# Moving loads, small steps and PSUM banks in a hand-ordered two-block transformer kernel

## The reference, cut to what matters

```python
def first_block(x, mem, ...):
    x = x + 0.5 * rmsnorm(swiglu(rmsnorm(x, g), ffn1), g_post)           # ffn1
    h = rmsnorm(x, mix_pre_g)
    proj = h @ w_in                     # q, k, v, z, xbc, dt, gates
    a = diff_attention(q, k, v) @ w_branch_attn
    s = (ssd(xbc, dt) gated by z, normed) @ w_branch_ssd
    x = x + rmsnorm((gates * (a, s)) @ w_mix_out, mix_post_g)            # mix
    x = x + rmsnorm(cross_attention(rmsnorm(x), mem) @ xa_w_o, xa_post_g) # xa
    return x + 0.5 * rmsnorm(swiglu(rmsnorm(x, g), ffn2), g_post)        # ffn2

def second_block(x, ...):
    proj = rmsnorm(x) @ w_in_2
    k_spec = rfft(filters made by a small sine network times a decay)    # from constants and weights
    u_hy = (hyena: gated long convolutions with k_spec, by FFT) @ w_hy_out
    u_attn = (attention with low-rank q and kv * silu(z)) @ w_attn_out
    merged = sigmoid(gate_hy) * u_hy + sigmoid(gate_attn) * u_attn
    return x + merged @ w_out
```

## Time and profile before

| | us |
|---|---|
| median of 3 runs | 1153.08 (1152.91 to 1153.16) |
| the profiled execution | 1152.91 |
| its span, first to last instruction | 1151.1 |
| TensorE busy in it | 1136.1 |
| VectorE busy | 774.7 |
| ScalarE busy | 589.3 |

### The profile page before, as it was taken

How to read it: one execution, slowest core, us unless ns; L and a number is a source line. 1 busy time by engine, 2 the same in 40 slices (tenths; PEclk the granted TensorE clock), 3 DMA queues, 4 the chain that set the end, 5 groups by cost and what they waited for, 6 DMA issues and landing times.

```text
span 1151.1 us, 21065 instructions
## 1 busy us (share of the span) xinstructions
PE 1136.1 (99%) x8564; PEld 1060.2 (92%) x8564; DVE 774.7 (67%) x1097; ACT 589.3 (51%) x846; POOL 0.2 (0%) x4
## 2 busy tenths in 40 slices
PE   7999999999999999999999999999999999999998
PEld 6999998999999999999999997999999699989898
DVE  5665555858898967786777746555555656984664
ACT  5544345557754335787445544444443466554361
POOL 0000000000000000000000000000000000000000
PEclk8999999999999999999999999999999999999999
DMA  7665555455443355444555333555555336443241
GB/s 284 239 217 183 182 182 182 167 200 184 153 177 110 111 170 179 147 142 157 182 199 203 106 134 128 188 199 177 190 193 182 105 132 241 147 146 110 73 147 38
DMA packets 29120, 189.62 MB, mean 165 GB/s; under 512 B 3480, under 2 KB 4793, under 8 KB 7226
## 3 DMA queue, kind: packets, MB, share of 16 engines
q1 hardware_dynamic: 26432, 180.89, 45.6%
q10 hardware_dynamic: 2618, 7.72, 2.0%
HBM read 187.55 MB, written 1.05 MB: 164 GB/s over the span
## 4 chain that ended last, share of the span: by engine, by line
PE 91%; DVE 5%; ACT 2%; issue 1%; DMA 1%; ACTq 0%; DVEq 0%
PE bank L457 26%; PE bank L459 26%; PE bank L458 26%; PE bank L535 3%; PE bank L912 2%; DVE sb_ssd_conv L2084 1%; PE bank L755 1%; PE bank L1093 1%; PE bank L1081 1%; DVE sb_w_lo L1874 1%; DMA sb_cols<-in_cols 1%; PE bank L899 1%; PE bank L1115 1%; PE bank L1138 1%; PE bank L975 0%
## 5 line engine op out<-in xcount | busy, mean ns | idle before, releaser
L1874 DVE TENSOR_TENSOR sb_w_lo<-sb_w_raw,sb_w_hi 128x2048 fp32r<-128x2048 f32 x169 | 386.5, 2290 | 179.5 <-ACT sb_w_hi L1224 179.4
L457 PE MATMUL bank<-sb_hT_hi,sb_w_hi 128*128 128x256 f32 x1576 | 447.5, 284 | 1.7 <-DVE sb_hT_lo L1957 1.7
L458 PE MATMUL bank<-sb_hT_lo,sb_w_hi 128*128 128x256 f32 x1576 | 440.3, 279 | 0.0
L459 PE MATMUL bank<-sb_hT_hi,sb_w_lo 128*128 128x256 f32 x1576 | 440.3, 279 | 0.0
L1224 ACT ACTIVATE sb_w_hi<-sb_w_raw 128x2048 fp32r<-128x2048 f32 x169 | 322.6, 1910 | 86.0 <-PE bank L459 84.5
L457 PEld LDWEIGHTS bank<-sb_hT_hi,sb_w_hi 128*128 128x128 f32 x1576 | 295.8, 188 | 6.4 <-issue 3.3
L458 PEld LDWEIGHTS bank<-sb_hT_lo,sb_w_hi 128*128 128x128 f32 x1576 | 295.5, 187 | 2.6 <-issue 1.4
L459 PEld LDWEIGHTS bank<-sb_hT_hi,sb_w_lo 128*128 128x128 f32 x1576 | 295.8, 188 | 0.0
L1281 ACT ACTIVATE sb_ffn_gate<-sb_ffn_gate 128x256 f32<-128x256 f32 x44 | 18.4, 418 | 149.0 <-DVE sb_ffn_gate L1972 149.0
L457 PE MATMUL bank<-sb_w_hi,sb_hT_hi 128*128 128x256 f32 x256 | 73.2, 286 | 0.7 <-DVE sb_hT_lo L2586 0.3
L458 PE MATMUL bank<-sb_w_lo,sb_hT_hi 128*128 128x256 f32 x256 | 71.1, 278 | 0.0
(11 more groups left out here) (406 smaller groups left out, 1748.4 us busy)
## 6 DMA issues: line engine op xcount, KB each, us to landing
sb_w_raw<-in_w SPq DMA_DIRECT2D x169, 1024.0 KB, 5.0
sb_w_raw<-in_w SPq DMA_DIRECT2D x4, 256.0 KB, 7.4
sb_w_raw<-in_w SPq DMA_DIRECT2D x2, 512.0 KB, 8.8
sb_mem_xn<-in_mem ACTq DMA_DIRECT2D x1, 1024.0 KB, 7.5
sb_post_g<-in_ffn_post_g ACTq DMA_DIRECT2D x2, 512.0 KB, 5.1
sb_dft_f<-in_c_dft ACTq DMA_DIRECT2D x1, 1024.0 KB, 6.7
out<-sb_x SPq DMA_DIRECT2D x4, 256.0 KB, 2.2
sb_x<-in_x SPq DMA_DIRECT2D x1, 512.0 KB, 3.9
```

The lines of the kernel that those rows point to most:

```text
L457: pe.matmul(o, a_hi, b_hi, start=first, stop=False)
L458: pe.matmul(o, a_hi, b_lo, start=False, stop=False)
L459: return pe.matmul(o, a_lo, b_hi, start=False, stop=last)
L1874: tt(w_lo[b % STAGES][:], w_raw[b % RING][:], f32(w_hi[b % STAGES][:]), ALU.subtract).then_inc(w_lo_in, 1)
```

## The change

Nothing is computed that was not computed before. Edits, by place:

- Start: the second half of `x` is loaded by SyncE right behind the first, ahead of the weights, and no longer by ScalarE ahead of `cols`; five warm-up matmuls in place of two.
- ffn1's end: two of the four banks of `norm_turn(1)` change places.
- mix: the first sine step moves behind the conversions of the mixed columns, on VectorE and ScalarE; the second moves into `out_part`, behind its second block, and its matmul behind `mix1`. The taps use banks 3, 4, 5, 6, 3, 4 in place of 3, 4, 5, 6, 2, 0, and `raw_turn(3)` claims 5, 6, 3, 4. On ScalarE the sum of squares for the next norm and the load of the post-norm gain move ahead of the sixth tap's copy.
- xa: `filter_decay` moves from ahead of the softmax into the `out_part` behind it, after its first and second block. On ScalarE the same two steps of the next norm move ahead of `spectrum(1)`.
- Last stage: `mla_turn(7)` moves from between the halves of `hyo0` to behind them; on ScalarE the first sigmoid moves ahead of the copy `mPT7`; on VectorE the block conversion moves ahead of `at_scale(3)` and the first `wide_gate`; on ScalarE the conversion of block `out1` moves behind the first of the four `fin` steps.

```diff
@@ tensor: start, ffn1's end
-                    norm_turn(1, mem_xn, 1, (7, 0, 2, 1))
+                    norm_turn(1, mem_xn, 1, (7, 0, 1, 2))
...
-            stay_warm(zeros[:, 0:P], zeros[:], 2)
+            stay_warm(zeros[:, 0:P], zeros[:], 5)
@@ tensor: mix
-                if i in (0, 2):
-                    filter_hidden(i // 2)
+                if i == 0:
+                    filter_hidden(0)
...
             token_pair(("mix0", "mix1"), FIRST["mix_out"], mixed_hi, mixed_lo, mixed_ready)
+            filter_hidden(1)
...
-            xq = FIRST["xa_q"]
             for i in range(6):
-                filter_taps(i, (3, 4, 5, 6, xq % 3, (xq + 1) % 3)[i])
-            raw_turn(3, x_added(1))
+                filter_taps(i, 3 + i % 4)
+            raw_turn(3, x_added(1), (5, 6, 3, 4))
             for i in (6, 7):
-                filter_taps(i, 7 if i == 6 else (xq + 2) % 3)
+                filter_taps(i, 7 if i == 6 else (FIRST["xa_q"] + 1) % 3)
@@ tensor: ffn2, last stage
-            filter_spectrum(2, (FIRST["ffn2"] + 2) % 3)
+            filter_spectrum(2, (FIRST["ffn2"] + 1) % 3)
...
-                             between=(lambda: at_turn(3, 7)) if i == 9 else lambda: mla_turn(7))
-                if 1 <= i < MLA_HEADS:
+                             between=(lambda: at_turn(3, 7)) if i == 9 else None)
+                if 1 <= i <= MLA_HEADS:
                     mla_turn(i - 1)
@@ scalar: start, mix, xa
-            act.dma_start(x[:, 1, :], a["x"][P:SEQ, :]).then_inc(S("x_in1"), 16)
...
-                if i == 0:
-                    hidden_sin(0)
             after(FIRST["attn_out"] + 3)
-            hidden_sin(1)
+            hidden_sin(0)
...
-            out_part("mix_out", "mix", 1)
+            def mix_between(i):
+                if i == 1:
+                    hidden_sin(1)
+
+            out_part("mix_out", "mix", 1, mix_between)
...
-            for i in range(6):
+            for i in range(5):
                 taps(i)
+            post_gain(2, POST[2])
+
+            norm_squares(x, xa_xn)
+            taps(5)
             norm_high(3, "xa_pre_g", hT_hi)
             for i in range(6, 8):
                 taps(i)
-            post_gain(2, POST[2])
-
-            norm_squares(x, xa_xn)
...
             spectrum(0)
+            post_gain(3, POST[3])
+
+            norm_squares(x, ffn[2]["xn"])
             spectrum(1)
             norm_high(4, "ffn2_pre_g", hT_hi)
-            post_gain(3, POST[3])
-
-            norm_squares(x, ffn[2]["xn"])
@@ scalar: last stage (the sigmoid's five lines, moved up, and this)
-            after(FIRST["at_out"])
             for i in range(4):
...
                 act.activation(hT_hi[:, 2 * i:2 * i + 2, :], mg2[:, 2 * i:2 * i + 2, :], ACT.Copy).then_inc(S("fin_hi"), 1)
+                if i == 0:
+                    after(FIRST["at_out"])
@@ vector: mix, xa (out_part calls between(i) behind low_after(FIRST[stage] + i))
-                if i == 0:
-                    hidden_arg(0)
             low_after(FIRST["attn_out"] + 3)
-            hidden_arg(1)
-            out_part("mix_out", "mix", 1)
+            hidden_arg(0)
+
+            def mix_between(i):
+                if i == 1:
+                    hidden_arg(1)
...
-            for t in range(TOK):
-                filter_decay(t)
...
-            out_part("xa_o", "xo", 2)
+            def xo_between(i):
+                if i < 2:
+                    filter_decay(i)
@@ vector: last stage
+                low_after(FIRST["gate2"] + i)
                 if i == 8:
                     at_scale(3)
 
                     dve.wait_ge(S("gate2"), 1)
-                    wide_gate(0, True)
-                low_after(FIRST["gate2"] + i)
-                if i == 9:
-                    wide_gate(1, True)
+                if i >= 8:
+                    wide_gate(i - 8, True)
@@ sync
-            sp.dma_start(x[:, 0, :], a["x"][0:P, :]).then_inc(S("x_in0"), 16)
+            for t in range(TOK):
+                sp.dma_start(x[:, t, :], a["x"][t * P:(t + 1) * P, :]).then_inc(S(f"x_in{t}"), 16)
```

More of the change, by code:

```diff
@@ L1340, in ffn_part, with out_part @@
                 after(down_at(n, PAIRS - 1))
-            def out_part(stage, key, i_post):
+            def out_part(stage, key, i_post, between=None):
                 for i in range(3):
@@ L1352, in out_part @@
                     after(FIRST[stage] + i)
+                    if between:
+                        between(i)
                 for t in range(TOK):
@@ L1817, in _ @@
                     read(ins, f"gg{i}")
+                if i >= 8:
+                    for j in range(8):
+                        wait_read(act, f"gg{j}")
+                    c = slice(8 * (i - 8), 8 * (i - 7))
+                    act.activation(gate2[:, c, :], gate2[:, c, :], ACT.Sigmoid).then_inc(S("gate2"), 1)
                 if i == 0:
@@ L1822, in _ @@
                     copy(f"mPT{i - 1}", m_PT[:], two(o))
-                if i >= 8:
-                    for j in range(8):
-                        wait_read(act, f"gg{j}")
-                    c = slice(8 * (i - 8), 8 * (i - 7))
-                    act.activation(gate2[:, c, :], gate2[:, c, :], ACT.Sigmoid).then_inc(S("gate2"), 1)
                 if i < MLA_HEADS:
@@ L2408, in _ @@
             xa_low(3)
-            out_part("xa_o", "xo", 2)
+            def xo_between(i):
+                if i < 2:
+                    filter_decay(i)
+            out_part("xa_o", "xo", 2, xo_between)
             norm_low(4, "ffn2_pre_g", hT_hi, hT_lo)
```

## The result

The changed kernel takes 1164.55 us (median of 4 executions, 1163.23 to 1166.01), the kernel before in the same comparison 1153.12 (1152.91 to 1153.86): ratio 1.0098, 95% interval 1.0081 to 1.0115. The prediction was 1164.4, range 1158.5 to 1168.0. The executions of the changed kernel spread over 2.8 us and the profiled one, at 1168.75, is slower than all four; those of before lie within 1 us. That spread is part of the result, and the profile shown is one from its upper end.

What follows compares the result with a forecast made beforehand. TensorE, busy 1136.1 of 1151.1 us, was taken as the bound, its idle time mostly at the start. -1.2 + 0 + 5.1 + 2.0 + 2.7 = +8.6, with clock +2.9 +11.5, on 1152.91: 1164.4, range 1158.5 to 1168.0.

Steps and rivals of the forecast that it cites:

- The mechanism: Start: with `cols` and x's second half loaded sooner, the first norm columns come at 8.6 in place of 9.82.
- 7.1 to 7.6: Start, a sign to look for: ScalarE's first rounding at these times in place of 9.29.
- The zeros' end at 7.25: Start: ten warm-up records end then if the granted clock rises at about 4.5 us; at 10 us if late.
- The term -1.2: Start: gain in us from earlier loads, less three more warm-ups; bounds -2.1 to +0.2.
- the predicted +5.1: mix: us from turnings of `raw_turn(3)` held by the sixth tap's late copy; range +1.6 to +5.6.
- the releaser named: mix, a sign: TensorE's turnings released by ScalarE's `sb_kfil`; release by VectorE's `sb_x` would favour the third rival.
- The third rival: mix and xa: sixth and second copies don't hold the turnings, no clock fall; +3.7 us, 1156.6; chance 0.10.
- 1.7 taken: mix: us for a fallen clock behind the wait ahead of `raw_turn(3)`, half of 3 us and a bit.
- the upper bound of 3.4: mix and xa: most that a fallen clock would cost behind each wait, in us; lower bound 0.
- +2.0 from the queue: xa: us from late writes of `x` and squares ahead of the `spectrum(1)` copy; from nothing to 2.5.
- The clock's 1.2: xa: us for a fallen clock behind a 2.9 us wait; bounds 0 and 3.4.
- The three terms: Last stage: `mla_out(7)` 0.8 late, `at_turn(3)` +2.0 in all, `out1`'s low part 0.65 more; sum +2.7, bounds +1.2 to +3.3.

Runs made afterwards that it cites:

- `start_all`: Kernel before with both start edits, the new order of loads and five warm-ups: 1152.08 us, ratio 0.9993.
- The two halves: Kernel before with both sine steps moved: 1155.4 us; kernel before with the taps' banks, claims, gain and squares moved, sine as before: 1159.72 us.
- the fill: Kernel before with the mix edits alone and four unread 128x512 matmuls in the wait ahead of `raw_turn(3)`: 1156.7 us, ratio 1.0036.
- `fill`: Whole changed kernel with eight unread 128x512 matmuls in the wait ahead of `raw_turn(3)`: 1165.52 us, ratio 1.0111.
- `last_low`: Kernel before with only VectorE's block conversion ahead of `at_scale(3)` and the `wide_gate` steps: 1156.19 us, ratio 1.0028.
- `last_all`: Kernel before with all the last stage's edits alone: 1155.02 us, ratio 1.0018.

## Why the prediction was right, and where it wasn't

The time was right to 0.2 us, and that is better than its terms were. By the isolated kernels' medians, against the prediction:

| place | predicted | measured |
|---|---|---|
| start | -1.2 | -0.8 |
| mix, waits and clock | 5.1 + 1.7 | +8.7 |
| xa, waits and clock | 2.0 + 1.2 | +2.3 |
| last stage | +2.7 | +2.2 |
| sum | +11.5 | +12.4 (whole: +11.4) |

- **Start.** The mechanism was right. The loads came early but later than worked out (ScalarE's first rounding at 7.92, set free by the weights, for 7.1 to 7.6). The zeros' end at 7.25 has three to four records at 0.85 us and the rest at half that, and how many there are differs between executions: the 6.22 us of `start_all` are four to five such records, with the zeros' end at 7.67 and the columns 1.0 early, and the 6.94 of the changed kernel's trace are six, with 8.40 and 0.29. PEclk shows 1.00 over both, and these counts are estimates from the lengths alone. The term -1.2 was measured as -0.8, and the order alone gave -1.0: the three warm-ups that the term counts with gained nothing. The base varies too: with the start of before, TensorE waited for `x` 0.7 to 2.3 us in nine traces, and 2.32 is the longest. The Trainium skill (DMA: Bandwidth & Descriptors, "Queues, rings and completion order") says that a DMA engine takes packets in turn from the queues that have work. By it the half, alone ahead of the weights, was to land with the first megabyte; the turnings at 6.36 agree.
- **mix, waits.** Right step by step: 2.84 us of `hidden_arg` behind the conversion, the sine, the squares and the rounding, the reduce 3.7 later in a trace that was 0.8 late already; then load, squares and copy, and the turnings at 639.43 for 633.58, less that 0.8: +5.0 for the predicted +5.1, by the releaser named. The two halves alone gave waits of 1.99 and 2.06. The third rival (the copies don't hold the turnings) falls by the releaser. (In the working, the second half's write ends at 636.6, where two thirds of 2.61 us behind 634.65 are 636.4.)
- **mix, clock.** The step was right, the size too small: 1.7 taken, 4.8 by the fill and 3.7 as what is left of 8.7 beyond the waits. I had scaled it by the start's length and halved it, and the upper bound of 3.4 has no row behind it: 6 us at half the clock cost 3. In the profiled executions the clock was at 0.50 for 10 us and more, and the price has two values some 3.7 us apart between executions.
- **xa.** +2.0 from the queue was right to 0.3, and the reason too: the decay alone doesn't do it. That the reordering alone costs as little was not tried. The clock's 1.2 there isn't in the median: +2.3 leaves 0.3 for it. It is not that the clock can't fall there: behind the same wait it did in one trace (`fill`) of three. The Trainium skill (TensorE: Matmul & The Clock Gate, "HAM oscillation") tells of a kernel in which the clock falls in every round of waiting for transfers, with waits of some 3 to 5 us. The prediction stretched that to both waits. The 4.2 us at mix agree; xa's 2.7 had it in one trace and not in two; and the falls behind 2.06 and 0.74 us came behind waits shorter than any in that example. What decides in a single execution stays open.
- **Last stage.** The three terms stood in order: 0.69 for the copy (0.8 predicted), 1.10 at the turning (1.2 predicted, 2.0 less 0.8), and out1's low part from 0.23 to 0.89 of waiting in the isolated kernel, +0.66 for the predicted 0.65 (in the changed kernel it was 1.3). The conversion alone cost by its median more than the whole group, which the prediction, adding the terms, had no row for.

So the two clock terms, 1.7 and 1.2, were too small a sum and in the wrong places: next to nothing at xa in the median, and 3.7 to 4.8 at mix. The 1.9 too little at mix was met in part by 0.9 too much at xa and 0.5 in the last stage, and the isolated sum is 1.0 above the whole, which is inside what medians of kernels with such a spread can tell. That all this came out at 0.2 us is luck.

## What to carry to other kernels

Follow a moved step through the in-order queue behind it, not only on its own engine: a late write cost 0.6 us, not clear of noise, while a copy was last, and 2.3 once the squares stood ahead of that copy. Behind a wait of 2 us the clock can fall and cost up to 5 us more, in some executions of a kernel and not in others; filling the wait with work whose result nobody reads brought most of that back. Time such edits one by one and in several executions, and set each execution's time beside its mean clock: two groups 3.7 us apart look like noise in a median of three.

## What the runs showed that I had not expected

- The clock fell for more than 8 us behind a wait of 2.06 us at mix and for 3 us behind 0.74. At xa, behind 2.69 or 2.70 with the same work around it, it didn't fall in two traces and fell for 3 us in a third. So neither the length of the wait nor the work beside it settles it alone.
- Without any fall of the granted clock, TensorE starts weight matmuls of 256 columns at two spacings. Those of `hyo0` stood 0.12 apart in `last_low` and 0.11 in `last_all`:

```profile
1107.76 0.28 PE L458 MATMUL bank<-sb_hy_lo,sb_w_hi 128*128 128x256 f32 x1
1107.88 0.28 PE L459 MATMUL bank<-sb_hy_hi,sb_w_lo 128*128 128x256 f32 x1
```

```profile
1107.41 0.28 PE L457 MATMUL bank<-sb_hy_hi,sb_w_hi 128*128 128x256 f32 x1
1107.52 0.28 PE L458 MATMUL bank<-sb_hy_lo,sb_w_hi 128*128 128x256 f32 x1
```

  Stretches of either kind are in every trace, at different places; what sets them stays open. At 0.118 and 0.114 apart, 50 us of such work would differ by 1.7 us; that is an estimate, and how much of the spread between executions it makes was not measured.
